# Bidirectional delta layer, one core: write strength in the decay's exponent, and the gate stage inside the projection

## What is computed

```python
g_f = -jnp.exp(a_log_fwd) * jax.nn.softplus(alpha_f + dt_bias_fwd)      # log decay, <= 0
bt_f = jax.nn.sigmoid(beta_f)                                           # write strength
# per head and chunk, gc = cumsum(g) inside the chunk
decay = jnp.where(incl, jnp.exp(gc_i - gc_j), 0.0)
kb, vb = k * beta[..., None], v * beta[..., None]
a = -jnp.where(strict, einsum(kb, k) * decay, 0.0)
tinv = inverse built from a, plus identity
u, w = tinv @ vb, tinv @ (kb * jnp.exp(gc)[..., None])
qk = einsum(q, k) * decay
q_dec, k_dec = q * jnp.exp(gc), k * jnp.exp(gc[-1] - gc)
chunk_decay = jnp.exp(gc[-1])
# scan over chunks
v_new = u - w @ state
o = q_dec @ state + qk @ v_new
state = state * chunk_decay + k_dec.T @ v_new
```

## Time and profile before

| | |
|---|---|
| median of 3 runs | 2455.64 us (2453.74 to 2458.28) |
| the profiled execution, its own time | 2452.92 us |
| its span, first to last instruction | 2451.3 us |
| TensorE busy | 2186.9 us, 89% of the span |
| VectorE busy | 1117.8 us, 46% |
| ScalarE busy | 658.4 us, 27% |
| GpSimd busy | 379.4 us, 15% |
| mean granted clock of TensorE | 0.958 |

### The profile page before, as it was taken

How to read it: one execution, slowest core, us unless ns; L and a number is a source line. 1 busy time by engine, 2 the same in 40 slices (tenths; PEclk the granted TensorE clock), 3 DMA queues, 4 the chain that set the end, 5 groups by cost and what they waited for, 6 DMA issues and landing times. The chain is left out here.

```text
span 2451.3 us, 29437 instructions
## 1 busy us (share of the span) xinstructions
PE 2186.9 (89%) x11392; PEld 1818.5 (74%) x11392; DVE 1117.8 (46%) x1874; ACT 658.4 (27%) x1000; POOL 379.4 (15%) x227
## 2 busy tenths in 40 slices
PE   6999999999999999999537999899985776899998
PEld 6788888888888888888426887788874443688887
DVE  7754335434344111221146777566652775522222
ACT  5511111111111011110034544444322554411111
POOL 4300000000000000000046565465500000000000
PEclk9999999999999999999768999999995999899999
DMA  6421222112122221221121222122005221743432
GB/s 225 163 104 52 77 77 77 65 63 82 72 77 77 77 69 59 77 77 52 38 82 59 78 78 78 62 78 78 18 13 172 61 78 53 273 155 137 155 137 86
DMA packets 81227, 219.94 MB, mean 90 GB/s; under 512 B 7489, under 2 KB 33217, under 8 KB 76913
## 3 DMA queue, kind: packets, MB, share of 16 engines
q1 hardware_dynamic: 71584, 183.55, 22.1%
q0 software_dynamic: 9552, 35.19, 3.7%
HBM read 174.02 MB, written 44.70 MB: 89 GB/s over the span
## 5 line engine op out<-in xcount | busy, mean ns | idle before, releaser
L73 PE MATMUL pr_acc<-x_hi,pr_w_lo 128*128 128x512 f32 (+1 forms) x1760 | 675.8, 384 | 26.1 <-DVE pr_w_lo L386 23.5
L74 PE MATMUL pr_acc<-x_lo,pr_w_hi 128*128 128x512 f32 (+1 forms) x1760 | 674.3, 383 | 0.0
L75 PE MATMUL pr_acc<-x_hi,pr_w_hi 128*128 128x512 f32 (+1 forms) x1760 | 674.2, 383 | 0.0
L73 PEld LDWEIGHTS pr_acc<-x_hi,pr_w_lo 128*128 128x128 f32 x1760 | 334.2, 190 | 91.4 <-issue 18.3
L74 PEld LDWEIGHTS pr_acc<-x_lo,pr_w_hi 128*128 128x128 f32 x1760 | 334.4, 190 | 63.6 <-issue 0.2
L75 PEld LDWEIGHTS pr_acc<-x_hi,pr_w_hi 128*128 128x128 f32 x1760 | 334.3, 190 | 63.7
L314 ACT ACTIVATE pr_w_hi<-pr_w_raw 128x1024 fp32r<-128x1024 f32 x118 | 124.8, 1059 | 758.0 <-PE pr_acc L75 739.3
L464 DVE TENSOR_TENSOR pr_padded<-pr_acc,pr_rstd 128x512 f32<-128x512 f32 x80 | 55.2, 692 | 501.5 <-PE pr_acc L75 501.4
L73 PE MATMUL ou_acc<-ou_w_hi,ou_m_lo 128*128 128x512 f32 x512 | 200.2, 391 | 18.0 <-DVE ou_w_lo L1721 18.0
L75 PE MATMUL ou_acc<-ou_w_hi,ou_m_hi 128*128 128x512 f32 x512 | 199.9, 390 | 0.0
L74 PE MATMUL ou_acc<-ou_w_lo,ou_m_hi 128*128 128x512 f32 x512 | 199.9, 390 | 0.0
(11 more groups left out here) (217 smaller groups left out, 2640.6 us busy)
## 6 DMA issues: line engine op xcount, KB each, us to landing
pr_w_raw<-in_w_in SPq DMA_DIRECT2D x118, 512.0 KB, 4.6
ou_w_raw<-in_w_out SPq DMA_DIRECT2D x32, 1024.0 KB, 4.8
proj_scratch<-pr_res POOLq DMA_DIRECT2D x51, 512.0 KB, 4.3
dl_qk<-proj_scratch SPq DMA_DIRECT2D x8, 1024.0 KB, 5.0
dl_grow<-gate_rows SPq DMA_DIRECT2D x8, 1024.0 KB, 7.1
dl_brow<-gate_rows SPq DMA_DIRECT2D x8, 1024.0 KB, 9.9
ou_x_in<-in_x SPq DMA_DIRECT2D x8, 1024.0 KB, 7.2
out<-ou_res POOLq DMA_DIRECT2D x8, 1024.0 KB, 4.7
```

Of the source, the lines that this page charges most:

```text
L73: pe.matmul(out, w_lo, x_hi, start=first, stop=False)
L74: pe.matmul(out, w_hi, x_lo, start=False, stop=False)
L75: return pe.matmul(out, w_hi, x_hi, start=False, stop=last)
```

## The change

Write strength: the four groups of columns now hold, in place of the sigmoid, its logarithm, which is the same softplus with the sign turned. `negc`, the bias of the decays' exponentials (L735), becomes that logarithm minus the sum, so that a matrix of decays carries the strength of the column it writes. With this `brow`, its load, `beta_keys`, `vb`, `hb`, `beg` and `beta_column` go. `keys_keys` is one call of 8 products in place of four calls of 4, for both directions at once; it stands ahead of the scan, and `matrix` of tiles 2 and 3 moves from scan step 3 to step 1. The half that scaled the values goes into ScalarE's copy, and the copied values get two buffers. `keys_keys` is what SyncE waits for before the next head's loads.

Gate stage: it goes as a block. The gate tile is number 46 and the four tiles of C's queries follow it. Its chain runs in the front stage on the freed tiles `padded`, `conv` and `kvs`; `T_GATE`'s tile is stored first and then overwritten. TensorE's turn to columns stands behind the last tile, and VectorE's copies behind that. The loads of the gate's constants and of `ident` move to the start of SyncE's list, and the store of the memory keys moves from SyncE to the head of GpSimd's stores.

```diff
@@ front_stage
-    STEPS = T_GATE // 2
-    SEGMENTS = ((T_A, 4, A_HEADS, "cccz"), (T_BQ, 2, 3, "pp"), (T_BZ, 2, 4, "zz"), (T_CQ, 2, 2, "pp"),
-                (T_GATE, 1, 1, "p"))
+    STEPS = TILES // 2
+    SEGMENTS = ((T_A, 4, A_HEADS, "cccz"), (T_BQ, 2, 3, "pp"), (T_BZ, 2, 4, "zz"), (T_GATE, 2, 1, "gp"),
+                (T_GATE + 2, 2, 1, "pp"), (T_GATE + 4, 1, 1, "p"))
+        gate_raw, gate_g, gate_pos = padded[:, 0, PAD:PAD + SEQ], padded[:, 1, PAD:PAD + SEQ], conv[:]
+        gate_sums = kvs[:].rearrange("p a n -> p (a n)")
...
-            sp.dma_start(kn[:], args["k_norm_c"]).then_inc(s_nw, 16)
+            sp.dma_start(norm_gate[:, 0:1], args["k_norm_c"]).then_inc(s_nw, 16)
+            sp.dma_start(small[:, 0:2], args["gate_consts"]).then_inc(g_in, 16)
+            sp.dma_start(c["ident"][:], args["ident"]).then_inc(g_in, 16)
             load_unit(2)
...
-            store_kv(4)
-            sp.wait_ge(s_kst, 80)
+            sp.wait_ge(g_rows, 2)
+            for group in range(2):
+                sp.dma_start(gate_rows[group], gate_sums[32 * group:32 * group + A_HEADS, :]).then_inc(g_st, 16)
+            sp.wait_ge(g_st, 32)
+            sp.wait_ge(s_kst, 64)
+            sp.wait_ge(s_nst, 16)
...
+            pool.wait_ge(s_kn, 1)
+            pool.dma_start(kv_scratch[:, 4:8], kvs[:]).then_inc(s_nst, 16)
+            def resets():
+                pool.wait_ge(g_x, 3)
+                pool.wait_ge(g_a, 2)
+                pool.memset(gate_raw, 1.0).then_inc(g_reset, 1)
+                pool.wait_ge(g_reset, 1)
+                pool.memset(gate_raw.rearrange("p (n i) -> p n i", i=CHUNK)[:, :, 0:1], 0.0).then_inc(g_reset, 1)
...
                     pool.sem_inc(s_left, 1)
+                    if kind == "g":
+                        resets()
...
+            pe.wait_ge(g_in, 32)
+            pe.wait_ge(g_rows, 2)
+            pe.wait_ge(g_x, 6)
+            pe.wait_ge(s_taken, 96)
+            for half in range(2):
+                for n_ in range(4):
+                    last = pe.transpose(acc[:, 6 + half, bass.ts(n_, P)], gate_sums[:, bass.ts(4 * half + n_, P)],
+                                        c["ident"][:])
+                last.then_inc(g_tr, 1)
...
+            def gate():
+                act.wait_ge(g_in, 32)
+                act.activation(small[:, 2:3], small[:, 1:2], ACT.Exp).then_inc(g_a, 1)
+                act.wait_ge(g_x, 2)
+                act.activation(gate_g, gate_raw, ACT.Abs).then_inc(g_a, 1)
+                act.wait_ge(g_a, 2)
+                act.activation(gate_g, gate_g, ACT.Exp, scale=-1.0).then_inc(g_a, 1)
+                act.wait_ge(g_a, 3)
+                act.activation(gate_g, gate_g, ACT.Ln, bias=c["one"][:, 0:1]).then_inc(g_a, 1)
...
+            def gate(t):
+                dve.wait_ge(g_in, 32)
+                dve.wait_ge(s_left, t + (1 + LEFT0))
+                dve.wait_ge(s_taken, t * 2 + 2)
+                dve.tensor_scalar(gate_raw[LOW, :], gate_raw[LOW, :], small[LOW, 0:1], None, ALU.add).then_inc(g_x, 1)
+                dve.tensor_scalar(gate_raw[HIGH, :], gate_raw[HIGH, :], -1.0, None, ALU.mult).then_inc(g_x, 1)
+                dve.wait_ge(g_x, 2)
+                dve.tensor_scalar(gate_pos, gate_raw, 0.0, None, ALU.max).then_inc(g_x, 1)
+                dve.wait_ge(g_a, 4)
+                dve.wait_ge(g_x, 3)
+                dve.tensor_tensor(gate_pos, gate_pos, gate_g, ALU.add).then_inc(g_x, 1)
+                dve.wait_ge(g_x, 4)
+                dve.tensor_scalar(gate_pos[LOW, :], gate_pos[LOW, :], small[LOW, 2:3], -1.0, ALU.mult,
+                                  ALU.mult).then_inc(g_x, 1)
+                dve.wait_ge(s_nst, 16)
+                dve.tensor_scalar(gate_sums[HIGH, :], gate_pos[HIGH, :], -1.0, None, ALU.mult).then_inc(g_x, 1)
+                dve.wait_ge(g_x, 6)
+                dve.wait_ge(g_reset, 2)
+                dve.tensor_tensor_scan(gate_sums[0:32, :], gate_raw[0:32, :], gate_pos[0:32, :], 0.0, ALU.mult,
+                                       ALU.add).then_inc(g_rows, 1)
+                dve.tensor_tensor_scan(gate_sums[32:64, ::-1], gate_raw[32:64, :], gate_pos[32:64, ::-1], 0.0,
+                                       ALU.mult, ALU.add).then_inc(g_rows, 1)
...
-                    if kind != "p":
+                    if kind == "g":
+                        gate(t)
+                    elif kind != "p":
...
             each_step(dve, step)
+            for half in range(2):
+                dve.wait_ge(g_tr, half + 1)
+                for group in range(4):
+                    src = acc[:, 6 + half].rearrange("p (n r) -> p r n", r=P)[:, 32 * group:32 * group + A_HEADS, :]
+                    dve.tensor_copy(cols[:, group, :, 4 * half:4 * half + 4], src).then_inc(g_cols, 1)
@@ delta_stage
-                sp.dma_start(grow[:], row_source(0, h)).then_inc(l_g, 16)
-                sp.dma_start(brow[:], row_source(2, h)).then_inc(l_b, 16)
+                sp.dma_start(grow[:], gate_rows[:, bass.ds(h, 1), :].rearrange("g a n -> (a g) n")
+                             .partition_broadcast(P)).then_inc(l_g, 16)
...
+                    act.activation(v_rows[:, parity, 4 * half:4 * half + 4],
+                                   pp[:, half].rearrange("p (a n) -> p a n", n=P), ACT.Copy, scale=0.5).then_inc(e_rows, 1)
...
-                for dst, src, scale in ((kbe, k_rows, beg), (kd, k_rows, kdc), (vb, v_rows, hb)):
+                for dst, src, scale in ((kbe, k_rows, egc), (kd, k_rows, kdc)):
...
                 neg_rows(g)
-                beta_keys(g)
                 decayed_queries(g, parity)
...
-                dve.tensor_tensor(kdc[:], glast[:], hc[:, 0:2], ALU.subtract).then_inc(e_dif, 1)
-                dve.tensor_scalar(negc[:], hc[:, 0:2], -1.0, None, ALU.mult).then_inc(e_col, 1)
-                dve.tensor_scalar(hb[:], hc[:, 2:4], 0.5, None, ALU.mult).then_inc(e_col, 1)
+                dve.tensor_tensor(negc[:], hc[:, 2:4], hc[:, 0:2], ALU.subtract).then_inc(e_dif, 1)
+                dve.wait_ge(e_dif, g * 2 + 1)
+                dve.tensor_tensor(kdc[:], glast[:], negc[:], ALU.add).then_inc(e_dif, 1)
...
-                dve.wait_ge(e_g, g * 4 + (b + 1))
+                dve.wait_ge(e_g, g * 4 + (2 * (b % 2) + 2))
...
-                    if more and level == 3:
-                        beta_column(g)
...
-                    if more and t == 3:
+                    if more and t == 1:
                         matrix(g, 2)
                         matrix(g, 3)
...
-            def keys_keys(g, b):
-                direction, half = divmod(b, 2)
-                pe.wait_ge(e_kb, g * 2 + (direction + 1))
+            def keys_keys(g):
+                for half in range(2):
                     pe.wait_ge(e_pt, g * 4 + (2 * half + 2))
+                    for i in range(4):
+                        cols_ = bass.ts(4 * half + i, P)
+                        last = pe.matmul(pp[:, half, bass.ts(i, P)], qk[:, 1, cols_], qk[:, 1, cols_],
+                                         start=True, stop=True)
+                    last.then_inc(e_g, 2)
...
                 if more:
-                    keys_keys(g, 0)
-                    keys_keys(g, 1)
+                    keys_keys(g)
                 for t in range(NC):
                     scan_step(h, parity, t)
-                    if more and t in (2, 3):
-                        keys_keys(g, t)
```

193 lines of the change are left out of this document (58 added, 135 removed).

## The result

| | before | after |
|---|---|---|
| median | 2456.46 us (4 runs, 2453.74 to 2458.28) | 2398.06 us (4 runs, 2393.08 to 2399.57) |
| the profiled execution, own time | 2452.92 | 2397.70 |
| its span | 2451.3 | 2395.9 |
| TensorE busy | 2186.9, 89% | 2176.7, 91% |
| VectorE busy | 1117.8 | 1082.7 |

The ratio is 0.976, with a 95% interval of 0.9742 to 0.9777: 58.4 us by the medians. The forecast was 2400, from 2388 to 2413. A right total can hide wrong terms, so I divide both executions at the same five marks: the first load of the constants, the delta stage's first load, the first products of the first head, the first load of the attention stage, and the output stage's first load of weights. Each was profiled twice, the second time in a later session (experiments 9 and 10).

The account below looks back on a forecast made before the run. TensorE bounds the front; in the heads only its stalls or own work can be won. Terms -33.9 - 4.7 - 17.8 + 0.9 + 0.3 = -55.2 take 2452.92 to 2397.7; with 2.7 for the median, 2400 us, range 2388 to 2413.

Parts of the forecast that it names:

- Gate stage: Between front and delta stage: its place of 33.6 us goes, plus 0.3 for the issue of `ident`; -33.9 us.
- The chain beside the last tiles: In the front's last tiles: the gate chain on VectorE delays no TensorE work, with some 18 us of cover; cost zero.
- End and start of the front: End: more semaphores to clear, +0.3 us. Start: two more small loads on SyncE ahead of weight units, +0.9 us.
- First preparation: Before the first head: GpSimd loses `vb`, 3.75 us, and VectorE's unit product shortens, 0.9; -4.7 us, bounds 3.7 and 6.
- Slots: The seven slots that prepare a next head: four edits and an earlier GpSimd inverse; -17.8 us, bounds 9 and 21.
- (a): In the slots' scan: keys by keys leaves two steps, 2 x 0.73 = 1.46 us won per slot.
- (b): In the slots' scan: `matrix` 2 and 3 move to step 1 without TensorE products beside them; 0.6 us lost.
- (c) and (d): In the slots: `beta_column` leaves level 3, 5.9 us won; `beta_keys` no longer slows the queries' unit product, 5.5 won.
- The heads give little: Rival: in the late scan steps GpSimd's mask rows or inverse slow VectorE; no heads gain, 2418 us; chance 0.15.
- Only moved: Rival: delta stage's first loads or barrier take up what the gate stage covered; half its place back, 2417; chance 0.03.
- Slower: Rival: the gate chain holds VectorE's list, so TensorE waits at tile 49; 2462 us at 100 of hold; chance 0.02.
- More than forecast: Rival: at the heads' loop return VectorE's 3.76 us without a releaser changes; -7.5, 2392.5 us, or plus as much; chance 0.10.

Follow-up runs that it names:

- experiments 9 and 10: The kernel before, then the kernel after, both unchanged and profiled once more: 2458.97 and 2395.34 us.
- experiment 1: Against the kernel after: old front, gate chain as a block of its own without reciprocals, then the new delta stage; 2419.69 us, ratio to before 0.9844.
- experiment 12: Kernel after plus six reciprocals with unused results on VectorE, in the gate chain ahead of its scans; 2415.29 us.
- experiment 7: Kernel after plus two GpSimd products of `vb`'s size ahead of the first inverse, results unused; 2405.67 us.
- experiment 6: Kernel after plus two GpSimd products of the size of `beta_keys`, beside the unit product, results unused; 2406.35 us.
- experiments 11: Kernel after plus three reciprocals with unused results on VectorE, in the gate chain ahead of its scans; 2398.59 us.
- experiment 2: Kernel after with keys by keys in four calls again, two inside the scan, and the last two matrices back at scan step 3; 2405.71 us.
- experiments 5: Kernel after plus one VectorE product of two small columns in level 3, result unused; 2402.68 us.
- experiment 4: Kernel after with both late matrices behind scan step 3 and keys by keys kept ahead of the scan; 2404.24 us.
- experiments 3: Kernel after with one late matrix behind scan step 1 and one behind step 2; 2397.45 us.
- experiment 8: Kernel after with late matrices split over scan steps 1 and 2, and VectorE's `end` moved from level 2 to levels 3 and 4; 2374.62 us, ratio to before 0.966.

## Why the prediction was right, and where its terms were off

- **Gate stage, -33.9.** Measured -34.4. Right. That 13.7 of it belong to the new form and 20.7 to the move was not separated in the prediction; experiment 1 did that.
- **The chain beside the last tiles, 0.** Right: no wait of TensorE, the chain's length 13.5 for 14.1. The cover was put at 18 us and is 23: the chain ended 17.8 us behind tile 46, for 20, and could have ended at 41, for 38.
- **End and start of the front, +0.3 and +0.9.** Next to nothing of the 1.2 shows. The constants' first load stands at 1205.58, 1206.68 and 1205.72 in the three profiles with the old front, and at 1205.29 to 1206.94 in the ten with the new one, experiment 12 left out; the means are 1206.0 and 1206.1, in profiles that differ by up to 1.6 among themselves. The step that failed is "the delay can pass through" by ScalarE's waits for raw weights; what absorbs two small loads there I did not test. The 5.3 us between the last store's landing and the constants is a slip: by the rows it is 1205.58 - 1201.65 = 3.9, which leaves the 0.3 inside its bounds.
- **First preparation, -4.7.** Measured -4.6, as 3.86 for the values (experiment 7) and 0.8 for the unit product (experiment 6).
- **Slots, -17.8.** Measured -22.2 to -22.7 in the two pairs of profiles, outside the term's own bound of 21 and the one term that was clearly mis-sized. The new delta stage, unchanged, took 518.50, 518.65, 520.33, 521.47 and 521.72 in the kernel after, its repeat and experiments 12, 1 and 11, so the gain is 19 to 23 and its excess over the forecast 1.5 to 5. The scans and gaps together vary by 0.6 in these five: they alone gave -10.5 for -6.4, which is most of the excess. (a) was right, 2.75 and 3.46 per step in experiment 2. (b), "1.42 and VectorE's next copy had 0.80 of idle before it: 0.6 lost", failed: it cost 0.30. I had the idle time right and the length wrong: each matrix takes 0.69 in both kernels, but the 1.42 held a pause of 0.04 ahead of the second one, and in the kernel after the second starts 0.08 before the first has ended, 1.28 in all. TensorE's own slack was not counted. (c) and (d) were about right, 5.7 for 5.9 and 6.0 to 6.3 for 5.5 (experiments 5 and 6); the inverses' -12.1, and -11.3 in the second pair, also hold falls of the clock that lie in different slots before and after. "Worth a few tenths at most" for GpSimd's earlier inverse was the worst sizing: the gaps lost 1.8 us, and 3.2 by experiment 4. The earlier end was noted, but what TensorE starts with at the end of the scan, exactly that tile, was not followed up.
- **Attention stage, 0.** Untouched, but its first profile before was 1 to 5 us below all others, so the comparison of two single spans (-55.4) hid the excess in the slots. That the profiled spans met the forecast of -55.2, and the median 2400 within 2 us, is luck in part: the changed stages gave 62.0, 6.8 more than forecast, and stages without a change gave back 6.6.
- **The signs of being wrong.** TensorE had no wait on low parts in the last tiles, and the copies stayed at 0.42 in the late scan steps. "A slot that stays above 66" did come: slot 3, with the loop's return, took 67.64, and the last slot, which prepares nothing, 67.75. Both were longer or as long before (70.55, 67.82), so the sign was too sharp for these two. The mean of 66.5 it was set by is short as well: the heads took 541.18 us and not the 532 of the stretch in the earlier trace rows, 67.6 per slot, and 64.8 after.
- **The rivals.** "The heads give little" fell on the copy at 0.42 beside L829. "Only moved" fell by the table of stretches: the delta stage took up nothing, it starts 34.4 us sooner and prepares faster. "Slower" fell by experiments 11 and 12, with its mechanism confirmed. "More than forecast" came true in part, though by the gaps and not by the loop's return: VectorE stood 2.80 us there for 3.76, and the gap of that slot went from 3.77 to 3.56.

## What to carry to other kernels

A chain that stands as a block between two stages can be hidden if its input is made a few tiles earlier; count the cover at the first thing queued behind it that the bounding engine needs, and try holds of different length to see how far off that point is. When work moves out of an ordered list, look at what is then the first thing that the next stage waits for: here an inverse that ended before the scan instead of after it was worth more than the slot's bookkeeping had it. And read the list of what the bounding engine waits for even where the change doesn't touch it: the largest entry was worth 22 us, in a few moved lines. Before a term is sized from one slot, see that the granted clock is the same in both kernels there: of the 1.07 us that slot 5 showed for the column, 0.9 stand at full clock, and the rest came with a fall of the clock.

## What was not expected of the hardware

**TensorE's clock falls after an idle of 2.1 to 2.6 us, in some slots and not in others.** The same 16 products, behind the same wait in level 3, in the kernel after:

```profile
1408.40 3.43 PE L1085 MATMUL dl_ring<-dl_dt,dl_wt 128*128 128x128 f32 x16 [2.64 <-DVE dl_wt L918]
...
1606.77 2.05 PE L1085 MATMUL dl_ring<-dl_dt,dl_wt 128*128 128x128 f32 x16 [2.64 <-DVE dl_wt L918]
```

and the granted clock of both stretches (columns as in the stretches above):

```profile
1408.40:1411.60 3.20, 3.20 (x16) 3.20 (x17) 2.37 (x7) 0.00 (x0) 3.20 (x2) 0.55 0.70 198
1606.70:1608.70 2.00, 1.93 (x16) 1.86 (x16) 2.00 (x8) 0.00 (x0) 2.00 (x2) 1.00 0.39 102
```

0.55 is near the lower of the two levels, 1.2 GHz, and 1.00 is 2.4 GHz. Of the slots with such a wait, 2 and 6 of the kernel after have the fall and 1, 3, 4 and 5 don't, and its repeat is the same; the last slot has it too, behind an idle of 2.05 us (3.55 us for the 16 products). The products take 1.4 to 1.5 us longer, and the slot pays 1.0 to 1.1: slot 2 has an inverse of 43.95, and 42.84 in experiment 12, without a fall. In experiments 1 to 7, 11 and 12 the same products took anything from 2.05 to 3.78 us, in other slots each time, though 1, 11 and 12 have the delta stage of after to the letter. This is what blurred the totals of experiments 3 to 7, and what experiment 8 removed together with the idle time: none of its eight slots has the fall there (1.95 us each). What decides in which slot the clock falls stays open. It isn't the code alone: in the kernel before slots 2, 4 and 5 have it in one profile and 2, 4 and 6 in the other. The delta stage began 1.0 us apart in these two (1244.57 and 1245.58), and 0.5 apart in the two of the kernel after (1209.88 and 1210.37), which agree; I did not test a shift alone.

**VectorE's copies out of PSUM don't mind GpSimd.** L950 took 0.411 to 0.426 us in all its 64 instances, with and without L829 beside it, while a small column with both inputs in SBUF took 1.00 beside GpSimd, for 0.18 in level 0. The Trainium skill, "SBUF — State Buffer", "Who interferes with whom", also has it that a VectorE instruction with at most one SBUF input, outside the two-port modes, doesn't contend with GpSimd. The trace agrees for this copy, which has none; I had weighed the rule on copies where this one applied.

**A stage with no change in it varied by 5 us.** The attention stage took from 241.7 to 247.0 us over all profiles, the shortest at a granted clock of 0.86 and the others at 0.81 to 0.84. The output stage took 369.3 to 371.5. The spans of two single profiles of this kernel can't be compared more closely than that; the stage that a change touches can.
